# A hybrid decoder trunk on one core: the fourth channel group of the depthwise convolution moves from GpSimd to VectorE

## What is computed

```python
def hybrid_mixer(h, w_in, ...):
    z = h @ w_in                                   # 7696 columns
    u_conv, sb_qkv, gq, gk, gv, gg, g_lr, gates = jnp.split(z, offs, axis=-1)
    y_a = conformer_conv(u_conv, ...)
    o_b = stick_breaking_attention(...)            # 8 heads, strictly causal
    o_c = gla_chunked(...)                         # 4 heads, chunks of 64 tokens
    ...
    return (g_a * y_a + g_b * y_b + g_c * y_c) @ w_o

def conformer_conv(u, w_dw, b_dw, ln_g, ln_b, w_out):
    a, g = jnp.split(u, 2, axis=-1)
    y = a * jax.nn.sigmoid(g)
    y = lax.conv_general_dilated(y, w_dw[:, None, :], window_strides=(1,),
        padding=((CONV_WIDTH - 1, 0),), feature_group_count=CONV_DIM, ...) + b_dw
    y = jax.nn.silu(layer_norm(y, ln_g, ln_b))
    return y @ w_out
```

## Time and profile before

| | |
|---|---|
| median of 3 runs | 1933.04 us (1932.81 to 1936.19) |
| the profiled execution's own time | 1936.59 us |
| its span in the trace | 1934.3 us |
| PE (TensorE) busy | 1824.0 us, 94% |
| DVE (VectorE) busy | 1553.7 us, 80% |
| ACT (ScalarE) busy | 1129.3 us, 58% |
| POOL (GpSimd) busy | 190.9 us, 10% |
| mixer of layer 0, projection to output | about 40 to 329 us of the span |
| mixer of layer 1 | about 559 to 840 us |
| mixture of experts | about 874 us to the end |

### The profile page before, as it was taken

How to read it: one execution, slowest core, us unless ns; L and a number is a source line. 1 busy time by engine, 2 the same in 40 slices (tenths; PEclk the granted TensorE clock), 3 DMA queues, 4 the chain that set the end, 5 groups by cost and what they waited for, 6 DMA issues and landing times.

```text
span 1934.3 us, 29139 instructions
## 1 busy us (share of the span) xinstructions
PE 1824.0 (94%) x10820; PEld 1595.9 (83%) x10821; DVE 1553.7 (80%) x1414; ACT 1129.3 (58%) x952; POOL 190.9 (10%) x156
## 2 busy tenths in 40 slices
PE   2999997899979999979999999999999999999997
PEld 2989997899969999877887787787877877878776
DVE  6998776999557667767888888888888888888886
ACT  4444564433354554645776767667767676677674
POOL 0394001000007800100000000000000000000000
PEclk7999999999989999989999999999999999999999
DMA  9965443799525333434988989979889899898892
GB/s 365 348 230 207 155 149 132 267 372 375 207 87 178 128 131 133 152 131 181 364 338 330 368 300 363 365 303 365 333 332 366 301 362 366 304 366 332 332 365 80
DMA packets 72524, 525.33 MB, mean 272 GB/s; under 512 B 8112, under 2 KB 8240, under 8 KB 8704
## 3 DMA queue, kind: packets, MB, share of 16 engines
q1 hardware_dynamic: 72288, 524.03, 72.0%
q0 software_dynamic: 160, 0.23, 0.0%
HBM read 523.17 MB, written 1.05 MB: 271 GB/s over the span
## 4 chain that ended last, share of the span: by engine, by line
PE 44%; DVE 9%; ACT 3%; issue 2%; DVEq 0%; ACTq 0%
PE bank L1591 24%; PE bank L1606 12%; DVE w_lo L1101 7%; ACT w_hi L728 3%; PE bank L1616 2%; PE bank L1626 2%; PE bank L1644 2%; PE bank L1333 1%; DVE arena L1235 1%; PE bank L1310 1%; PE bank L1561 0%; DVE arena L895 0%; DVE arena L917 0%; DVE arena L921 0%; DVEq L1233 0%
## 5 line engine op out<-in xcount | busy, mean ns | idle before, releaser
L1101 DVE TENSOR_TENSOR w_lo<-raw,w_hi 128x2048 fp32r<-128x2048 f32 x224 | 512.9, 2290 | 85.9 <-ACT w_hi L728 64.1
L728 ACT ACTIVATE w_hi<-raw 128x2048 fp32r<-128x2048 f32 x224 | 428.4, 1916 | 126.2 <-PE bank L1606 77.0
L1333 PE MATMUL bank<-acts,w_hi 128*128 128x256 f32 x2080 | 378.8, 286 | 37.3 <-DVE acts L908 30.7
L1333 PEld LDWEIGHTS bank<-acts,w_hi 128*128 128x128 f32 x2080 | 326.8, 194 | 41.2 <-issue 33.0
L1591 PE MATMUL bank<-acts 128*128 128x512 f32 x1248 | 305.1, 393 | 0.0
L1591 PE MATMUL bank<-w_hi,acts 128*128 128x512 f32 x960 | 300.4, 394 | 1.3 <-DVE acts L1247 1.3
L1333 PE MATMUL bank<-acts,w_lo 128*128 128x256 f32 x1040 | 295.2, 284 | 0.0
L1101 DVE TENSOR_TENSOR acts<-raw,acts 128x2048 fp32r<-128x2048 f32 x112 | 256.3, 2289 | 32.4 <-ACT acts L728 29.0
L1591 PEld LDWEIGHTS bank<-acts 128*128 128x128 f32 x1248 | 233.6, 188 | 52.9
L1606 PE MATMUL bank<-w_hi,acts 128*128 128x512 f32 x832 | 263.1, 397 | 0.0
L728 ACT ACTIVATE acts<-raw 128x2048 fp32r<-128x2048 f32 x112 | 214.8, 1917 | 72.9 <-PE bank L1591 70.5
(11 more groups left out here) (229 smaller groups left out, 2120.3 us busy)
## 6 DMA issues: line engine op xcount, KB each, us to landing
raw<-in_experts SPq DMA_DIRECT2D x336, 1024.0 KB, 4.8
raw<-in_stream SPq DMA_DIRECT2D x161, 1024.0 KB, 5.6
arena<-in_x_t SPq DMA_DIRECT2D x1, 1024.0 KB, 11.8
out_t<-arena SPq DMA_DIRECT2D x2, 512.0 KB, 2.6
arena<-in_c_row SPq DMA_DIRECT2D x1, 512.0 KB, 4.3
arena<-in_vecs SPq DMA_DIRECT2D x1, 224.0 KB, 2.7
arena<-in_glr_w POOLq DMA_DIRECT2D x2, 64.0 KB, 4.1
arena<-in_a POOLq DMA_DIRECT2D x2, 32.0 KB, 4.3
```

The source lines that it names most:

```text
L728: act.activation(w_hi[s], raw[:, slot, :], ACT.Copy).then_inc(hi_written, 1)
L1101: dve.tensor_tensor(w_lo[s], raw[:, slot, :], f32(w_hi[s]), ALU.subtract).then_inc(lo_written, 1)
L1333: mm = pe.matmul(out[:, c, :], w[:, 256 * k + P * c:256 * k + P * c + P], (hi if high else lo)[:, k, :], start=(k == 0 and n == 0 and c == 0),
```

## The change

GpSimd's function `taps` and its calls go, with the two semaphores `pool_conv_taps` and `pool_conv_products`. VectorE's `taps` runs over four groups instead of three, and the fourth has the same start as the third (first = 6). TensorE's `conv_sums` no longer waits for GpSimd's taps. Everything else is as it was.

```diff
-        conv_taps, pool_taps, scans = sem("conv_taps"), sem("pool_conv_taps"), sem("scans")
-        pool_products = sem("pool_conv_products")
+        conv_taps, scans = sem("conv_taps"), sem("scans")
...
-            def taps(layer, k0, k1):
-
-                for k in range(k0, k1):
-                    w = vec(layer, "conv_dw")[:, TAPS * 3 + k:TAPS * 3 + k + 1]
-                    src, acc, product = ypad[:, 3, k:k + T], conv_acc[:, 3, :], conv_tmp[:, k % 2, :]
...
-                    pool.tensor_scalar(product, src, w, None, ALU.mult).then_inc(pool_products, 1)
-                    products[0] += 1
-                    pool.wait_ge(pool_products, products[0])
-                    pool.wait_ge(pool_taps, TAPS * layer + k)
-                    pool.tensor_tensor(acc, acc, product, ALU.add).then_inc(pool_taps, 1)
...
                 pool.memset(ypad[:, :, 0:TAPS - 1], 0.0).then_inc(pad_zeroed, 1)
-                wait_read(pool, ("z", layer, 3, 0))
-                taps(layer, 0, TAPS)
-
                 pool.wait_ge(sc_copied, 2 * (layer + 1))
...
                 for n in range(2):
-                    for c in range(3):
-                        first = (4, 4, 6)[c]
+                    for c in range(4):
+                        first = (4, 4, 6, 6)[c]
...
                 pe.wait_ge(ready, value)
-                pe.wait_ge(pool_taps, TAPS * (layer + 1))
```

More of the change, by code:

```diff
@@ L462, in _ @@
             pool.affine_select(one_or_zero[:, :], ones, [[-1, P]], ALU.is_equal, 0.0, 0, 1).then_inc(mask_written, 1)
-            products = [0]
-            def taps(layer, k0, k1):
-                for k in range(k0, k1):
-                    w = vec(layer, "conv_dw")[:, TAPS * 3 + k:TAPS * 3 + k + 1]
-                    src, acc, product = ypad[:, 3, k:k + T], conv_acc[:, 3, :], conv_tmp[:, k % 2, :]
[L470 to L475, removed]
-                    pool.tensor_scalar(product, src, w, None, ALU.mult).then_inc(pool_products, 1)
-                    products[0] += 1
-                    pool.wait_ge(pool_products, products[0])
-                    pool.wait_ge(pool_taps, TAPS * layer + k)
-                    pool.tensor_tensor(acc, acc, product, ALU.add).then_inc(pool_taps, 1)
             for layer in range(DEPTH):
```

## The result

The changed kernel takes 1946.36 us (median of 4 runs, 1944.77 to 1948.45); the kernel before took 1933.02 us beside it. The ratio is 1.0064, 95% interval 1.0052 to 1.0077: slower, by 13 us. The forecast was slower, by 6.4 us, and its range ended at 1943.2 us. So the direction is right and the size is not. The two profiled executions differ by less than the medians: their spans are 1934.3 and 1944.6 us, 10.3 us apart. The one before took 3.6 us more than its median (1936.59 against 1933.0), the one after took its median (1946.37). What is read from the two traces adds up to 10.3, not to 13.3.

What follows compares the result with a forecast made beforehand. In layer 0's front TensorE waits for VectorE, and later in both layers `gla_out` waits for `gla_states`. Terms -3.6 + 3.2 + 2.8 + 4.0 = +6.4 us on 1933.0 gave 1939.4 us, range 1934.4 to 1943.2 us.

Steps and rivals of the forecast that it cites:

- GpSimd's taps slow VectorE; taking them away pays at the front of layer 0: Up to unit 10's low part VectorE gets back 5.2 us and pays 1.6 for four extra taps: -3.6 us.
- Seven exposed taps at each end: Units 22 to 25, ahead of `gla_states`: seven unhidden taps, 2.8 us; with 0.4 left from units 18 to 21, +3.2 in layer 0.
- The fronts and the middle of layer 1 cost nothing: Layer 1 up to unit 21: time won is worth 0 and extra taps cost 0, because VectorE waits for ScalarE.
- TensorE's clock, +4.0 us: Stops ahead of `gla_out` of 4.3 and about 3.7 us each bring a stretch at 1.2 GHz, 2.0 us each.
- Behind the mixers nothing changes: Stages after the mixers: later waits move as they are; the +6.4 us is put onto the median of 1933.0 us.
- That the clock holds: Rival at the stops ahead of `gla_out`: clock stays up at one or both, 1935.4 to 1937.4 us; chance 0.25.
- The hidden taps: Rival: the 14 taps of units 22 to 25 hide in the wait of `gla_out`, 1929.8 us; chance 0.1.
- Transfers: Rival at the front: DMA transfers take VectorE's place, so it gives nothing; +10.0 us, 1943.2 excluded no part, 1943.0 us; chance 0.08.

Runs made afterwards that it cites:

- experiment 4: The change in one layer at a time, GpSimd keeping its taps in the other: layer 1 alone 1942.66 us, layer 0 alone 1936.34 us.
- experiment 7: Changed kernel with taps of units 24 and 25 behind `gla_states`: 1927.71 us; kernel before with VectorE's six taps of unit 25 behind it: 1931.38 us.
- experiment 1: Changed kernel with 35 (layer 0) and 30 (layer 1) unneeded matmuls run by TensorE while it waits ahead of `gla_out`: 1933.15 us.
- experiment 2: Changed kernel with 17 and 14 unneeded matmuls in TensorE's waits ahead of `gla_out`, leaving stops of 2.47 and 2.23 us: 1935.8 us.
- experiment 6: Changed kernel with the eight taps of unit 25 behind `gla_states` instead of ahead of it, in both layers: 1927.41 us.
- experiment 5: Changed kernel without group 3 of the convolution, computed by neither GpSimd nor VectorE: 1929.64 us.

## Why the forecast had the direction and missed the size

- *GpSimd's taps slow VectorE; taking them away pays at the front of layer 0, -3.6 us.* Right: unit 10 starts 3.7 us earlier, the first wait and unit 9's slow clock are gone, the second wait is 0.97 us. A tap at 0.40 and a low part at 2.29 us held in both layers, an ada half at 1.19 in layer 0. One execution of the kernel before gave the clock's part of this term, and another would have given more. In two other traces with GpSimd's taps in layer 0 (layer 1 alone in experiment 4, the reordered kernel before in experiment 7) the two stops were 2.3 and 2.5 us, the clock fell at the second, and the work behind unit 10 started at 114.95 and 115.52 us instead of 113.48; in the changed kernel it starts at 109.55.
- *Seven exposed taps at each end, +3.2 and +2.8 us.* Right: stops of 4.5 and 3.9 us were measured where 4.3 and 3.7 stood. In layer 1 `gla_out` would have to be 2.8 us later relative to the start of the layer; it starts 5.7 us later in the span, and unit 0 of that layer starts 3 us later, which leaves 2.7. In layer 0 `gla_out` is 1.4 us earlier than before, where the two terms together had 0.4.
- *The fronts and the middle of layer 1 cost nothing.* Right: no wait of TensorE for VectorE there.
- *TensorE's clock, +4.0 us.* This is the step that failed: the term was mis-sized. The mechanism and both places were right, the price was 4.8 + 6.0 = 10.8 us at the two places alone, and the filler of experiment 1 gave it back. I took 1.3 and 2.6 us from two stops of 2.9 and 3.0 us and called 2.6 each the bound from above. Nothing bounded it. What follows the stops to come is forty small matmuls, not a unit of large ones, and after 4.5 and 3.9 us the clock stayed down for 10.2 and 13.7 us instead of three to seven. Length alone does not make that: before, a stop of 4.7 us stood ahead of layer 1's unit 0, and its 48 large matmuls took 7.9 us, 2.1 us over the 5.8 of a unit at the full clock:

```profile
559.40:567.30 7.90, 7.90 (x48) 0.68 0.01 2
```

The trace of before also has a stop of 3.9 us with small matmuls (the expert router's) behind it, and its window shows a PEclk of 0.51 for 9.8 us; as a row for the upper bound it would have been the right one:

```profile
858.70:868.50 9.80, 9.80 (x48) 0.51 0.01 2
```
- *Behind the mixers nothing changes, and the profiled execution's surplus of 3.6 us goes onto the median.* Not quite. Without the clock's term the span should have grown by 2.4 us, and with its clock restored (experiment 1) the changed kernel's span was 1934.0 us, 0.3 less than before: at layer 1's sums it was 1.8 us behind, and the rest of the program gave 2.1 back. One place for it is the output projection of layer 1. Behind the stop of 3.0 us ahead of it PEclk was 0.54 over 6.6 us before, and behind a stop of 2.8 us in experiment 1 it was 0.74, which is worth 0.7 us:

```profile
815.70:822.30 6.60, 6.56 (x43) 0.74 0.41 161
```

So later stops keep their length, nearly, but not always their price. The stretch from layer 1's sums to the end holds the same work in all twelve kernels; it took 1180.7 us in the trace of before, the longest of all, and 1176.7 to 1180.4 in the others. So up to 4 us of a total seem to be a matter of the execution, not of the kernel. By the medians the miss is 13.3 - 6.4 = 6.9 us, and the clock's term alone was short by 6.8. That these agree so closely is partly luck: between the two traces the change is 10.3 us, with the clock 6.8 over its term and the other terms and the later stages together 2.9 under theirs.
- *Rivals.* That the clock holds was wrong for this kernel; it held once the stops were filled, and a stop of 2.24 us left it up in experiment 2. The hidden taps come true once the order is changed (experiment 6); the condition that I named, that `gla_states` does not stand behind the taps, is what the two edited lines make. Transfers never took VectorE's place.

## What to carry to other kernels

Before work goes from an idle engine to a busy one, look for the next result of the busy engine that somebody waits for: here an instruction of 0.4 us ahead of it in the queue cost 0.4 us, and behind it nothing. A stop of TensorE of more than about two microseconds should be priced with the clock as a chance: between 2.1 and 3.3 us it fell in some executions and not in others, at 3.9 us and more each time. The price should be read from a place with the same kind of work behind it, and from more than one execution. For a stop that can't be avoided, unneeded matmuls on data that lie ready were a cheap cure here. And two engines can be slower side by side than one of them alone: here the fused instruction on VectorE took less than a quarter of the time of GpSimd's pair (0.40 against 1.83 us), and VectorE's other instructions got faster as well.

## What the runs showed of the hardware that I had not expected

- The loss behind a stop comes as a step, and between 2.1 and 3.3 us the length does not tell whether it comes. Stops of 1.8 us or less left the clock up. Of 37 stops between 2.1 and 3.3 us, 27 brought it down (the shortest 2.15 us, in the trace of before) and 10 did not (the longest 3.00 us, with the change in layer 0 alone). All of 3.9 us or more brought it down. What decides in between is open.
- At the two stops ahead of `gla_out` the clock stayed low for 10.2 and 13.7 us with small fp32 matmuls behind them (10.2 in each of the two runs with one layer changed), and for 6.8 us in both places when 24 matmuls of 128x256 came first. Behind a stop of 2.47 us it was 6.8 us with small ones too.
- Beside GpSimd's taps a tap of VectorE took 662 ns on average instead of 480 (experiment 5, the same three groups without them), an ada half 1396 instead of 1218 and a low part 2474 instead of 2292.
